# Three passes over groups of tokens become three phases over all tokens, and GpSimd normalises the probabilities

## The chip, the cores and the metric

One core of a Trainium2 chip. The metric is the device time of one execution in microseconds, the median of the runs shown.

## What is computed

One inference step of a one-layer streaming encoder in fp32: 2048 new frames of a prompt and 64 of a sample stream, model width 1024. 17 row tiles: 16 of 128 frames and one of 64.

```python
z = rms_norm(x, norm_mix) @ w_in            # 1024 -> 1408: u 256, q 768, k 192, v 192
d = trailing_means(u, (2, 4, 8, 16)) - u    # one window for each 64 channels
pool_o = (d @ w_pool_of_group) * pool_scale
q, k = rms_norm(q, q_norm), rms_norm(k, k_norm)        # by head of 64
s = q @ k.T / 8 - slope * abs(distance)     # 12 heads, 3 kv heads, 192 keys a chunk of 64
p = exp(s - m); p = p / (sum(p) + exp(sink - m))       # m = max(s, sink)
h = x + concat(pool_o, p @ v) @ w_out       # 1024 -> 1024
hn = rms_norm(h, norm_ffn)
y = h + (silu(hn @ w_gate) * (hn @ w_up)) @ w_down     # 1024 -> 2816 -> 1024
```

The last 15 rows of u and 128 rows of k and v are outputs too.

## The kernel before

Each fp32 operand of a large product is split in two fp32r numbers, high and low, and `split_products` (L601 to L603) issues three matmuls: high by high, high by low, low by high. ScalarE makes the high part of a weight block (`high1`, `high2`, L962, L967, L973), GpSimd the low part (`low`, L521), each for a block of 128 x 1024.

The tokens are cut in three parts of 768, 768 and 576 (`NT`, 6, 6 and 5 tiles). A part goes through everything before the next begins. `boundary` normalises its rows (ScalarE sums of squares, L991 to L995; VectorE scaling, L1325), transposes them on TensorE (L615) and splits them. `slab_unit` multiplies 11 slabs of `w_in` with the weights stationary and half the tokens of the part (384 or 288) moving, so that queries and keys come out transposed. Their sums of squares over a head are matmuls with a block of ones (`head_sums`, L679, L683, L684), values are transposed back (L658). Pooling windows are sums on GpSimd (L546, L550), mapped by `pool_map` (L742).

`attend` runs through the units (kv head g, tile t) in an order written out by hand. Of a unit: `scores` (L698), bias and maximum on VectorE (`softmax_top`, L1458 to L1473), exponentials with their sums on ScalarE (`exps`, L1108, L1110), sum, reciprocal and product on VectorE (`normalised`, L1483 to L1488), `prob_transposes` (L711), `weighted_values` (L727). Between the units lie late query slabs and tiles of the out projection (`out_tile`), whose products of 512 columns are added to `h` by VectorE (L1337).

The feed-forward is 11 groups of 256 columns of the hidden layer. A group is eight gate and up products of 24 matmuls (weights stationary, 384 or 288 tokens moving) and a down product with activations stationary and 512 columns of `w_down` moving: six matmuls for each full tile and half, four for the sample tile. Every part loads and splits all weights anew. Loads are issued by SyncE, stores of `h` by ScalarE.

## Time and profile before

| | before |
|---|---|
| median of 3 runs | 2288.44 us (2283.53 to 2292.7) |
| the profiled execution, its own time | 2288.89 us |
| its span | 2287.1 us |
| busy TensorE / VectorE / ScalarE / GpSimd | 97% / 41% / 32% / 27% |
| granted TensorE clock, mean | 0.99 |

The page lists the busy time of each engine (PE is TensorE, PEld its weight load, DVE VectorE, ACT ScalarE, POOL GpSimd, SP SyncE). A group line names a line of the kernel, the engine and operation, out<-in with shapes, the count, busy time and mean, and the idle time before them with what ended it. Matmuls are pipelined: one lasts longer than the step from its start to the next start. A window line gives for a stretch its length, the busy time of each engine with the count of instructions, the granted clock, and what the DMA engines moved.

### The profile page before, as it was taken

The numbers are of one execution on the slowest core, as the hardware profiler recorded it, in microseconds if no ns is written. First come the engines' busy times: TensorE is split into PE (matmuls) and PEld (weight loads), VectorE is DVE, ScalarE is ACT, GpSimd is POOL, SyncE is SP. The second block draws the span as 40 slices with busy tenths as digits, with TensorE's granted clock in tenths as the row PEclk, the third lists the DMA queues.
The fourth block names the chain that finished last, engine by engine and source line by source line (L and its number), as shares of the span: only waits on it lengthen the run. The fifth ranks groups of instructions, "written<-read, shape, count | busy, mean of one in ns | idle before, by whom it ended". The sixth has DMA issues, their size and how long they took to land.

```text
span 2287.1 us, 32537 instructions
## 1 busy us (share of the span) xinstructions
PE 2219.1 (97%) x12823; PEld 1998.9 (87%) x12823; DVE 948.6 (41%) x1589; ACT 726.0 (32%) x1570; POOL 625.2 (27%) x278
## 2 busy tenths in 40 slices
PE   7999999999999999999999999999998999999999
PEld 6876899999999989767999999999886689999998
DVE  3478613322222344786123322222557653434244
ACT  4565422121121235653212121121365342222221
POOL 2320333232232213102423232232132124333331
PEclk9999999999999999999999999999999999999999
DMA  4100232212112033002322212111321223223221
GB/s 135 47 34 20 90 99 61 68 55 73 55 55 92 19 129 102 19 20 92 96 70 64 65 56 73 55 58 53 115 94 38 82 74 102 83 74 91 73 74 42
DMA packets 194793, 159.94 MB, mean 70 GB/s; under 512 B 7421, under 2 KB 177322, under 8 KB 194698
## 3 DMA queue, kind: packets, MB, share of 16 engines
q1 hardware_dynamic: 191742, 149.55, 21.0%
q10 hardware_dynamic: 2956, 9.08, 1.0%
q8 instruction: 66, 1.08, 0.2%
q14 instruction: 29, 0.24, 0.0%
HBM read 149.63 MB, written 9.07 MB: 69 GB/s over the span
## 4 chain that ended last, share of the span: by engine, by line
PE 86%; DVE 8%; ACT 3%; issue 1%; DMA 1%; POOL 1%; SPq 0%; DVEq 0%; ACTq 0%
PE ps L601 27%; PE ps L602 26%; PE ps L603 26%; PE ps L727 2%; DVE xn L1325 1%; DVE s_sb L1458 1%; PE ps L698 1%; DVE negmax L1466 1%; PE ps L711 1%; DVE h L1337 1%; POOL w_lo L521 1%; ACT s_sb L1108 1%; DVE xt_lo L1316 1%; ACT xn L991 1%; PE ps L615 1%
## 5 line engine op out<-in xcount | busy, mean ns | idle before, releaser
L521 POOL TENSOR_TENSOR w_lo<-raw,w_hi 128x1024 fp32r<-128x1024 f32 x249 | 593.4, 2402 | 1571.4 <-ACT w_hi L973 961.5
L601 PE MATMUL ps<-xt_hi,w_hi 128*128 128x384 f32 (+1 forms) x2640 | 861.1, 326 | 4.0 <-DVE h L1337 1.9
L602 PE MATMUL ps<-xt_lo,w_hi 128*128 128x384 f32 (+1 forms) x2640 | 854.7, 324 | 0.0
L603 PE MATMUL ps<-xt_hi,w_lo 128*128 128x384 f32 (+1 forms) x2640 | 854.6, 324 | 0.0
L601 PEld LDWEIGHTS ps<-xt_hi,w_hi 128*128 128x128 f32 x2640 | 498.7, 189 | 13.0 <-issue 6.4
L602 PEld LDWEIGHTS ps<-xt_lo,w_hi 128*128 128x128 f32 x2640 | 498.7, 189 | 2.2
L603 PEld LDWEIGHTS ps<-xt_hi,w_lo 128*128 128x128 f32 x2640 | 498.3, 189 | 0.0
L1337 DVE TENSOR_TENSOR h<-ps,h 128x512 f32<-128x512 f32 (+1 forms) x510 | 349.8, 689 | 262.5 <-PE ps L603 261.2
L1555 DVE TENSOR_TENSOR aa<-ps,sg 128x384 f32<-128x384 f32 (+1 forms) x132 | 69.2, 524 | 826.7 <-PE ps L603 824.9
L601 PE MATMUL ps<-w_hi,act_hi 128*128 128x512 f32 x704 | 278.6, 396 | 0.0
L603 PE MATMUL ps<-w_hi,act_lo 128*128 128x512 f32 x704 | 277.8, 395 | 0.0
L602 PE MATMUL ps<-w_lo,act_hi 128*128 128x512 f32 x704 | 277.8, 395 | 0.0
L1195 ACT ACTIVATE sg<-ps 128x384 f32<-128x384 f32 (+1 forms) x132 | 61.4, 465 | 665.0 <-PE ps L603 664.9
L973 ACT ACTIVATE w_hi<-raw 128x1024 fp32r<-128x1024 f32 x150 | 150.5, 1049 | 65.0 <-PE ps L603 34.4
L967 ACT ACTIVATE w_hi<-raw 128x1024 fp32r<-128x1024 f32 x60 | 60.2, 1051 | 340.9 <-PE ps L603 248.2
L603 PEld LDWEIGHTS ps<-w_hi,act_lo 128*128 128x128 f32 x704 | 132.0, 187 | 31.9
L601 PEld LDWEIGHTS ps<-w_hi,act_hi 128*128 128x128 f32 x704 | 132.0, 188 | 30.2
L602 PEld LDWEIGHTS ps<-w_lo,act_hi 128*128 128x128 f32 x704 | 132.0, 188 | 30.2
L1568 DVE TENSOR_TENSOR act_lo<-aa,act_hi 128x384 fp32r<-128x384 f32 (+1 forms) x132 | 124.2, 941 | 2.8
L1108 ACT ACTIVATE s_sb<-s_sb,negmax 128x192 f32<-128x192 f32 (+1 forms) x198 | 86.7, 439 | 64.0 <-DVE esink L1473 63.6
L1209 ACT ACTIVATE act_hi<-aa 128x384 fp32r<-128x384 f32 (+1 forms) x132 | 64.8, 491 | 119.3 <-DVE aa L1555 119.3
L601 PE MATMUL ps<-w_hi,xt_hi 128*128 128x512 f32 x192 | 79.9, 416 | 4.0 <-POOL w_lo L521 4.0
(139 smaller groups left out, 1719.2 us busy)
## 6 DMA issues: line engine op xcount, KB each, us to landing
raw<-in_w_gate SPq DMA_DIRECT2D x66, 512.0 KB, 3.8
raw<-in_w_up SPq DMA_DIRECT2D x66, 512.0 KB, 3.9
raw<-in_w_down SPq DMA_DIRECT2D x66, 512.0 KB, 3.2
...
```

What stands on the lines that cost most here:

```text
L521: nc.gpsimd.tensor_tensor(lo, raw, hi.bitcast(F32), ALU.subtract).then_inc(done, 1)
L601: nc.tensor.matmul(out, w_hi, m_hi, start=first, stop=False)
L602: nc.tensor.matmul(out, w_hi, m_lo, start=False, stop=False)
L603: return nc.tensor.matmul(out, w_lo, m_hi, start=False, stop=last)
L967: nc.scalar.activation(w1_hi[:, c], raw1[:, c], ACT.Copy).then_inc(hi_done, 1)
L973: nc.scalar.activation(w2_hi[:, n], raw2[:, n], ACT.Copy).then_inc(hi_done, 1)
L1108: nc.scalar.activation(p, p, ACT.Exp, bias=negmax[:, b, e, c:c + 1], accum_out=den[:, b, e, c:c + 1])
L1195: nc.scalar.activation(sg[:, n % 2, 0:s.NB], ps[:, bank0 if n == 0 else 4 + n % 2, 0:s.NB], ACT.Silu).then_inc(silu_done, 1)
L1209: nc.scalar.activation(act_hi[:, parity, n // 2, (n % 2) * s.NB:(n % 2 + 1) * s.NB], aa[:, n % 2, 0:s.NB], ACT.Copy).then_inc(ah_done, 1)
L1337: nc.vector.tensor_tensor(out, ps[0:rows, bank, :], out, ALU.add).then_inc(d_free, 1)
L1555: nc.vector.tensor_tensor(aa[:, n % 2, 0:s.NB], ps[:, bank0 if n == 0 else 6 + n % 2, 0:s.NB], sg[:, n % 2, 0:s.NB], ALU.mult).then_inc(a_ ...
L1568: nc.vector.tensor_tensor(act_lo[at], aa[:, n % 2, 0:s.NB], act_hi[at].bitcast(F32), ALU.subtract).then_inc(al_done, 1)
```

## The change

The kernel is written anew around three phases.

Mixer phase, over all 17 tiles, with `w_in` held in SBUF, loaded and split once, and scaled by `norm_mix` there. The transposed tokens of a tile are stationary and weights move: 256 columns for u (`pool_columns`), and 384 for the queries, key and value of one kv head (`group_columns`), the u columns once a tile and the others once a unit. 51 units in the order of `UNITS`, in 55 steps: in step n TensorE projects unit n, transposes the queries and key of n-1, multiplies values of n-4, scores n-1, and transposes probabilities of n-3. Head sums are a reduction on VectorE, the normalising is done on rows. The trailing means are products with constant bands (`pool_means`). Row sums of x for a later tile stand at the head of ScalarE's step. The division: VectorE forms sum and reciprocal, GpSimd multiplies. The mixer output is stored to DRAM, with rows of 512 bytes.

Out phase, by tile: load the mixer output and x, split, multiply with `w_out` (which takes the place of `w_in`, loaded once), add, store h, normalise, transpose and store the result to DRAM.

Feed-forward phase, in three parts of 704 tokens: moving halves of 352, five tiles of 128 rows and one of 64 in each part. Both tokens and h are loaded from DRAM; the groups and the splitting of weights are as before, each part again with all weights.

The core of the diff:

```diff
-NT = (6, 6, 5)
-TILE0 = (0, 6, 12)
-TMAX = 6 * PART
...
+NTILES = 17
+SAMPLE = 16
+QCOLS = 4 * HD
+GCOLS = QCOLS + 2 * HD
+TILE_SETS = [(0, 1, 2)] + [(t,) for t in range(3, 14)] + [(14, 15, 16)]
+UNITS = [(g, t) for tiles in TILE_SETS for g in range(N_KV) for t in tiles]
...
+HALF_AT = {t: (3 * t - 2, 3 * t - 1) for t in range(3, 13)} | {t: (2 * t + 10, 2 * t + 11) for t in range(13, 17)}
+STEPS = NU + 4
...
+PARTS = 3
+T = TOKENS // PARTS
+NB = T // 2
...
-            def head_sums(s, oi):
-                need(pe, ss_free, oi)
-                if s.whole(oi):
-                    pe.wait_ge(sq_ready, oi + 1)
-                    nc.tensor.matmul(ps[:, 2, 0:s.NB], headsum[:, :], sq[:, oi % 2, 0:s.NB],
-                                     start=True, stop=True).then_inc(ss_ready, 1)
-                    return
-                pe.wait_ge(sq_low, s.splits(oi) + 1)
-                nc.tensor.matmul(ps[:, 2, 0:s.NB], headsum_r[:, :], sq_hi[:, 0:s.NB], start=True, stop=False)
-                nc.tensor.matmul(ps[:, 2, 0:s.NB], headsum_r[:, :], sq_lo[:, 0:s.NB],
-                                 start=False, stop=True).then_inc(ss_ready, 1)
...
-            def normalised(s, n):
-                t = s.units[n][1]
-                ai, chunks = s.a0 + n, s.chunks(t)
-                b = ai % 3
-                dve.wait_ge(e_ready, ai + 1)
-                link(nc.vector.tensor_tensor(den[:, b, :, 0:chunks], den[:, b, :, 0:chunks], esink[:, b, :, 0:chunks],
-                                             ALU.add))
-                link(nc.vector.reciprocal(rden[:, b, :, 0:chunks], den[:, b, :, 0:chunks]))
-                for c0, c1, k0 in s.spans(t):
-                    p = s_sb[:, b, :, KEYS * c0:KEYS * c1].rearrange("p e (c k) -> p e c k", k=KEYS)[:, :, :, k0:]
-                    last = nc.vector.tensor_tensor(
-                        p, p, rden[:, b, :, c0:c1].unsqueeze(3).to_broadcast([PART, 2, c1 - c0, KEYS - k0]), ALU.mult)
-                last.then_inc(p_ready, 1)
...
+            def load_mixed(i):
+                slot = (NTILES + i) % 3
+                if i < 3:
+                    sp.wait_ge(z_ready, ZG[UNIT[2, NTILES + i - 3]] + 1)
+                else:
+                    sp.wait_ge(out_ready, 2 * (i - 3) + 2)
+                for r, count in stored_at(i):
+                    sp.wait_ge(o_stored[r], 16 * count)
+                rows = rows_of(i)
+                load(xt_raw[:, slot, :, 0:rows], mix_k[:, :, PART * i:PART * i + rows], mix_loaded[i % 3])
...
+            def normalised(n):
+                t, b = UNITS[n][1], n % 3
+                pool.wait_ge(rden_ready, n + 1)
+                for c0, c1, k0 in spans(t):
+                    p = s_sb[:, b, :, KEYS * c0:KEYS * c1].rearrange("p e (c k) -> p e c k", k=KEYS)[:, :, :, k0:]
+                    last = nc.gpsimd.tensor_tensor(
+                        p, p, rden[:, b, :, c0:c1].unsqueeze(3).to_broadcast([PART, 2, c1 - c0, KEYS - k0]), ALU.mult)
+                last.then_inc(p_ready, 1)
+            for n in range(NU):
+                normalised(n)
+                for i in range(2):
+                    if n == 1:
+                        scale_group(2, i)
+                    if n == 2:
+                        wg_low(2, i)
+                for part, unit in enumerate([UNIT[g, SAMPLE] for g in (0, 0, 1)]):
+                    if n == unit + 1:
+                        for c in ((0, 1), (2, 3, 4), (5, 6, 7))[part]:
+                            wo_low(c)
+                if n >= NU - 2:
+                    mix_low(n - NU + 2)
+            mix_low(2)
...
+            def split_products(out, s_hi, s_lo, m_hi, m_lo, first, final):
+                nc.tensor.matmul(out, s_hi, m_hi, start=first, stop=False)
+                nc.tensor.matmul(out, s_lo, m_hi, start=False, stop=False)
+                return nc.tensor.matmul(out, s_hi, m_lo, start=False, stop=final)
...
+            def project(zi, t, w_hi, w_lo, cols, split):
+                out = bank_of_z(zi)[0:rows_of(t), 0:cols]
+                pe.wait_ge(tp_free, TP["x", t, 1] + 1)
+                rows, slot = rows_of(t), t % 3
+                for k in range(KT):
+                    if t == 0:
+                        pe.wait_ge(split, k + 1)
+                    last = split_products(out, xt_hi[:, slot, k, 0:rows], xt_lo[:, slot, k, 0:rows], w_hi[:, k],
+                                          w_lo[:, k], k == 0, k == KT - 1)
+                last.then_inc(z_ready, 1)
...
+            def query_transposes(n):
+                rows = rows_of(UNITS[n][1])
+                bank = tp_bank(("q", n))
+                pe.wait_ge(qn_ready, n + 1)
+                for i in range(3):
+                    last = nc.tensor.transpose(bank[:, rows * i:rows * (i + 1)], qn[0:rows, n % 2, PART * i:PART * (i + 1)],
+                                               ident[0:rows, 0:rows])
+                last.then_inc(tp_ready, 1)
...
+            def pool_means(t):
+                rows = rows_of(t)
+                pe.wait_ge(u_free, t + 1)
+                if t == 1:
+                    pe.wait_ge(band_loaded, 16)
+                need(pe, b3_free, B3["mean", t])
+                before = 3 if t == SAMPLE else (t - 1) % 3
+                for b in range(2):
+                    for e in range(2):
+                        i = 2 * b + e
+                        out = ps[HD * e:HD * (e + 1), 3, PART * b:PART * b + rows]
+                        f = slice(HD * i, HD * (i + 1))
+                        last = nc.tensor.matmul(out, u_sb[:, t % 3, f], band[:, i, 0:rows], start=True, stop=t == 0)
+                        if t > 0:
+                            last = nc.tensor.matmul(out, u_sb[:, before, f], prev[:, i, 0:rows], start=False, stop=True)
+                last.then_inc(b3_ready, 1)
...
+            def out_half(i, nh):
+                rows, slot = rows_of(i), (NTILES + i) % 3
+                pe.wait_ge(mix_split, i + 1)
+                if i == 0:
+                    pe.wait_ge(qn_ready, NU)
+                need(pe, out_free, 2 * i + nh - 1)
+                out, cols = ps[0:rows, nh], slice(512 * nh, 512 * (nh + 1))
+                for c in range(KT):
+                    if i + nh == 0:
+                        pe.wait_ge(wo_split, c + 1)
+                    hi, lo, _ = wo(c)
+                    last = split_products(out, xt_hi[:, slot, c, 0:rows], xt_lo[:, slot, c, 0:rows], hi[:, cols],
+                                          lo[:, cols], c == 0, c == KT - 1)
+                last.then_inc(out_ready, 1)
...
+            pe.wait_ge(ident_loaded, 16)
+            for t in range(3):
+                for half in range(2):
+                    x_transposes(t, half)
+                pool_columns(t)
+            cache_transposes()
+            pe.wait_ge(const_loaded, 16 * N_CONST)
+            for n in range(STEPS):
+                if n < NU:
+                    if n > 0:
+                        for t in pool_before(n):
+                            pool_columns(t)
+                    group_columns(n)
+                else:
+                    out_half((n - NU) // 2, (n - NU) % 2)
+                if 1 <= n <= NU:
+                    query_transposes(n - 1)
+                if n >= 4:
+                    weighted_values(n - 4)
+                if 1 <= n <= NU:
+                    scores(n - 1)
+                for e in step_events(n)[1]:
+                    if e[0] == "map":
+                        pool_map(e[1])
+                if 3 <= n < NU + 3:
+                    prob_transposes(n - 3)
+                for e in step_events(n)[1]:
+                    if e[0] == "mean":
+                        pool_means(e[1])
+                for e in step_events(n)[0]:
+                    if e[0] == "x":
+                        x_transposes(*e[1:])
+                if n >= STEPS - 2:
+                    x_transposes(NTILES, n - STEPS + 2)
+            for i in range(2, NTILES):
+                for nh in range(2):
+                    out_half(i, nh)
+                    x_transposes(NTILES + i - 1, nh)
+            for n in range(4):
+                for which in range(2):
+                    gate_up_unit(0, n // 2, n % 2, which)
+                if n < 2:
+                    x_transposes(2 * NTILES - 1, n)
+            pe.wait_ge(out_free, 2 * NTILES)
+            pe.wait_ge(tp_free, len(TP_EVENTS))
+            for G in range(1, NG):
+                gate_up(G)
+                down(G - 1)
+            down(NG - 1)
...
+            for n in range(STEPS):
+                for t in HALF_AT:
+                    if x_step(t) == n:
+                        x_rstd(t)
+                if 0 < n < NU:
+                    for t in pool_before(n):
+                        pool_copy(t)
+                if n < NU:
+                    squares(n)
+                if 1 <= n <= NU:
+                    query_copy(n - 1)
+                if n < NU:
+                    value_copy(n)
+                    head_rstd(n)
+                if n >= 4:
+                    output_copy(n - 4)
+                for e in step_events(n)[1]:
+                    if e[0] == "map":
+                        map_copy(e[1])
+                if 3 <= n < NU + 3:
+                    prob_copy(n - 3)
+                for e in step_events(n)[1]:
+                    if e[0] == "mean":
+                        means_copy(e[1])
+                for e in step_events(n)[0]:
+                    if e[0] == "x":
+                        x_high(*e[1:])
+                if n in (1, 2, 4, 5):
+                    wg_highs(1 + n // 4, (n - 1) % 3)
+                for part, unit in enumerate([UNIT[g, SAMPLE] for g in (0, 0, 1)]):
+                    if n == unit + 2:
+                        wo_highs(part)
+                if NU - 1 <= n < NU + 2:
+                    mix_highs(n - NU + 1)
+                if 1 <= n <= NU:
+                    exps(n - 1)
+                if n == STEPS - 2:
+                    h_rstd(0)
+                if n >= STEPS - 2:
+                    stage_copy(0, n - STEPS + 2)
+            for i in range(2, NTILES + 1):
+                h_rstd(i - 1)
+                if 3 <= i + 1 < NTILES:
+                    mix_highs(i + 1)
+                if i == 4:
+                    high2(0, range(4))
+                if 9 <= i < NTILES:
+                    xb_highs(0, i - 9)
+                for half in range(2):
+                    stage_copy(i - 1, half)
...
+            for n in range(STEPS):
+                for t in HALF_AT:
+                    if x_step(t) == n:
+                        x_norm(t)
+                if 0 <= n - 2 < NU:
+                    normalised(n - 2)
+                if n < NU:
+                    head_sums(n)
+                    normed(n)
+                else:
+                    out_add((n - NU) // 2, (n - NU) % 2)
+                if 1 <= n <= NU:
+                    softmax_top(n - 1)
+                for e in step_events(n)[0]:
+                    if e[0] == "x":
+                        x_low(*e[1:])
+                if n in (1, 2):
+                    wg_lows(1, n - 1)
+                if n == STEPS - 2:
+                    h_norm(0)
...
+            def normalised(n):
+                t = UNITS[n][1]
+                b, nch = n % 3, chunks(t)
+                dve.wait_ge(e_ready, n + 1)
+                link(nc.vector.tensor_tensor(den[:, b, :, 0:nch], den[:, b, :, 0:nch], esink[:, b, :, 0:nch], ALU.add))
+                nc.vector.reciprocal(rden[:, b, :, 0:nch], den[:, b, :, 0:nch]).then_inc(rden_ready, 1)
...
```

## Rows read from the trace of the kernel before

**Rows 1.** the page, part 1: busy time of each engine

```profile
PE 2219.1 (97%) x12823; PEld 1998.9 (87%) x12823; DVE 948.6 (41%) x1589; ACT 726.0 (32%) x1570; POOL 625.2 (27%) x278
```

**Rows 2.** timeline of TensorE in feed-forward groups: start us, us, engine, line

```profile
359.62 0.34 PE L601 MATMUL ps<-xt_hi,w_hi 128*128 128x384 f32 x1
...
392.90 0.39 PE L601 MATMUL ps<-w_hi,act_hi 128*128 128x512 f32 x1
...
409.70 0.34 PE L601 MATMUL ps<-xt_hi,w_hi 128*128 128x384 f32 x1
...
2099.91 0.30 PE L602 MATMUL ps<-xt_lo,w_hi 128*128 128x288 f32 x1
...
2100.84 0.30 PE L603 MATMUL ps<-xt_hi,w_lo 128*128 128x288 f32 x1
```

**Rows 3.** groups by line and form: count, busy us, mean ns, idle before

```profile
L601 PE MATMUL ps<-xt_hi,w_hi 128*128 128x384 f32 x1760 | 598.2, 340 | 2.4 <-issue 1.2 <-DVE h L1337 1.1
...
L601 PE MATMUL ps<-w_hi,act_hi 128*128 128x512 f32 x704 | 278.6, 396 | 0.0
...
L601 PE MATMUL ps<-xt_hi,w_hi 128*128 128x288 f32 x880 | 262.9, 299 | 1.7 <-DVE h L1337 0.8 <-issue 0.6 <-POOL w_lo L521 0.2
```

**Rows 4.** timeline of TensorE, one unit of attention between out products

```profile
1001.61 0.92 PE L698 MATMUL ps<-kt_sb,qt_sb 64*128 64x192 f32 x8
1002.46 0.87 PE L711 MATMUL ps<-ident,s_sb 128*128 128x128 f32 x6
1003.27 1.39 PE L727 MATMUL ps<-pt_sb,v_sb 64*64 64x128 f32 x16
1004.59 0.50 PE L601 MATMUL ps<-w_hi,xt_hi 128*128 128x512 f32 x1
```

**Rows 5.** timeline of TensorE, a whole head sum and what follows it

```profile
109.22 0.91 PE L679 MATMUL ps<-sq,headsum 128*128 128x384 f32 x2
109.97 0.60 PE L711 MATMUL ps<-ident,s_sb 128*64 128x128 f32 x4
```

**Rows 6.** windows: length, busy (count) of PE PEld DVE ACT POOL, PEclk, DMA, GB/s

```profile
0.00:295.00 295.00, 267.50 (x1588) 226.13 (x1589) 172.37 (x316) 150.82 (x389) 64.44 (x38) 0.98 0.22 68
1630.00:1880.00 250.00, 225.42 (x1492) 189.49 (x1491) 150.65 (x299) 119.81 (x334) 57.99 (x27) 0.96 0.26 83
128.00:138.00 10.00, 10.00 (x47) 8.46 (x48) 7.81 (x22) 5.72 (x23) 2.18 (x1) 0.53 0.28 105
10.00:20.00 10.00, 5.62 (x24) 4.70 (x24) 8.13 (x8) 7.40 (x17) 6.16 (x4) 1.00 0.81 259
```

**Rows 7.** timeline of the start

```profile
3.96 1.06 ACT L991 ACTIVATE xn<-h 128x1024 f32<-128x1024 f32 x1 [1.78 <-DMA h<-in_x_prompt]
...
5.47 0.20 ACT L995 ACTIVATE rstd<-ss 128x1 f32<-128x1 f32 x1
...
10.69 1.94 PE L615 MATMUL ps<-ident,xn 128*128 128x128 f32 x8 [10.69 <-DVE xn L1325]
...
12.30 1.28 DVE L1325 SCALAR_TENSOR_TENSOR xn<-h,rstd,g_mix 128x1024 f32<-128x1024 f32 x1 [1.76 <-ACT rstd L995]
...
14.80 2.35 POOL L521 TENSOR_TENSOR w_lo<-raw,w_hi 128x1024 fp32r<-128x1024 f32 x1
...
14.89 3.34 DVE L1325 SCALAR_TENSOR_TENSOR xn<-h,rstd,g_mix 128x1024 f32<-128x1024 f32 x1
```

**Rows 8.** timeline of one softmax on VectorE and ScalarE

```profile
1008.54 1.14 DVE L1458 SCALAR_TENSOR_TENSOR s_sb<-dist,slope,ps 128x384 f32<-128x384 f32 x2 [0.17 <-PE ps L698]
...
1011.10 0.46 ACT L1108 ACTIVATE s_sb<-s_sb,negmax 128x192 f32<-128x192 f32 x1
...
1012.87 0.19 ACT L1110 ACTIVATE esink<-esink 128x4 f32<-128x4 f32 x1
```

**Rows 9.** groups by line and form, the low part on GpSimd and the normalising

```profile
L521 POOL TENSOR_TENSOR w_lo<-raw,w_hi 128x1024 fp32r<-128x1024 f32 x249 | 593.4, 2402 | 1571.4 <-ACT w_hi L973 961.5 <-ACT w_hi L962 343.3 <-ACT w_hi L967 266.3
...
L1488 DVE TENSOR_TENSOR s_sb<-s_sb,rden 128x768 f32<-128x768 f32 x45 | 48.1, 1069 | 1.6
```

2043 lines of the change are left out of this document (831 added, 1212 removed).

## The prediction

> **What bounds the kernel now.** I read the page first: TensorE is busy for 2219.1 us of the span of 2287.1, and no other engine reaches half of it [rows 1]. So the end is set by the TensorE stream, and two things are wanted: what the stream needs, and what is lost in it. Busy time is no measure of need, since matmuls overlap; the step from one start to the next is. In a feed-forward group of parts 1 and 2, 192 matmuls of 384 columns run from 359.62 to 392.90 and 72 of 512 columns from there to 409.70, without an idle record between them [rows 2]: 173.3 and 233.3 ns each. In part 3 seven steps of 288 columns take 0.93 us, 133 ns. The line through 288 and 384 is 0.42 ns a column plus 12.5 ns; it gives 160 ns at 352 and 120 ns at 256 columns (estimates). The counts are those of the grouping by form [rows 3], each for one of three products.
>
> By these steps the feed-forward of before needs 22 groups of 50.1 us and 11 of 38.7 (192 x 133 ns + 56 x 233.3 ns): 1527.8 us. The other 759 us are three mixers with out projection. Their stream: 1056 x 173.3 + 528 x 133 ns = 253 us of projection, 800 x 233.3 ns = 187 us of out projection; attention, by one step of tile and group: scores, probability transposes, weighted values from 1001.61 to 1004.59, 2.98 us [rows 4], 45 full units and 6 smaller ones (2.4 and 1.55 us) 146 us; 34 row tiles of eight transposes at some 0.93 us (six take 0.81), 32 us; head sums of 0.75 us a whole unit of 384 columns [rows 5], 27 whole and 21 split ones, 26 us; pooling map, value and state transposes, some 15 us. Sum 2186. So about 101 us are lost. In the windows over the mixers TensorE is idle for 27.5 us in part 1 and 24.6 in part 3, and its granted clock is 0.98 and 0.96 on the mean, 0.53 from 128 to 138 us, which is the 1.2 GHz level after short pauses [rows 6]. The feed-forward loses nothing. A better time can only come from these 101 us, and each new matmul costs its step.
>
> **The change part by part: the stream.** Feed-forward, gate and up: 6336 matmuls of 352 columns instead of 4224 of 384 and 2112 of 288, 1014 us each way; nothing. Down: five full tiles and one of 64 rows in each part are 68 matmuls a group, 33 x 68 = 2244 against 2200: +10.3 us. Out projection 17 x 48 = 816 against 800, since the sample tile loses its short form: +3.7. Projection: tokens are now stationary and weights move, 51 x 24 of 384 columns and 17 x 24 of 256: 212.1 + 49.0 = 261.1 us, +8; the sample tile pays full columns. Queries and keys come out in rows, so the head-sum matmuls go (-26) and so do value and state transposes (-6.5), and three transposes a unit come: six take 0.81 us [rows 4], so 0.43 x 51 = +22. Pooling means move from GpSimd to eight small matmuls a tile, half of the sixteen that take 1.32 us [rows 4], with the switch 0.75 x 17 = +13. The map costs the same. Together the stream is 2186 + 25 = 2211 us.
>
> One rule of the Trainium skill speaks on the steps. "TensorE: Matmul & The Clock Gate", section "Back-to-back issue gap", gives columns / 2.4 + 2.5 ns for a single warm matmul and says that real streams are set by weight load and matmul together. The row shows 173.3 ns at 384 columns where the formula has 162.5, so the measurement decides; by the formula the 256-column matmuls would take 109 instead of 120 ns, and the sum would be 4.5 us lower.
>
> **What is lost in the new stream.** (a) Start. Now TensorE starts at 10.69 us, because the first row scaling waits for a broadcast weight [rows 7]; the new one needs none (the weight goes into w_in), so the transposes can start near 7. But then ScalarE has, in order, three row sums of 1.7 us (3.96 to 5.67), 8 + 8 weight copies, and copies of transposes, and VectorE the same number of low parts. By their durations the first group matmul comes at some 28 us, of which 11 are needed: 17 lost (12 to 25, as the copies overlap or not). The loads for it, 4 MB, take about 16 us at the 259 GB/s of rows 6 and lie beside it. (b) Filling the pipeline over nine steps, with group 1 and 2 weights still being split: 7. (c) Steady steps. The loop is scores, bias and maximum on VectorE (2.52 us from 1008.54), exponentials on ScalarE (1011.10 to 1013.06) [rows 8], then in ScalarE's order the squares of the next unit (0.4), the query copies (0.6), scores (0.97): 6.5 us, and 7.0 when the normalising of queries, which VectorE now does ahead of the bias, is late. TensorE needs 7.6 us a step (24 x 173.3 ns + 0.43 + 2.98) and 28 for a tile's three steps with pooling, so it covers the loop. Once a tile the row sum of a later tile (1.7 us) and its scaling (1.28) stand at the head of a step: 9.5 us against 8. Some 1 us a tile, 14 in all; bounds 0 (pool columns cover it) and 45 (3 us a tile, if durations add end to end instead of overlapping by 0.09 us as between copies). (d) The end of the mixer. Five w_out splits of 0.96 us stand ahead of the exponentials of one step, three of another: 6. The first low part of the stored mixer output is queued on GpSimd behind the multiply of unit 49, whose divisors need scores, bias and exponentials of that unit: 4.5 + 0.4 + 1.5 + 2.4 us after its scores, while TensorE is ready after 0.8: 8 lost. Bounds 3 and 25. (e) Out phase. A tile is 11.2 us of products and 1 of transposes; 2 MB go and come in it (mixed rows, residual, two stores), 164 GB/s. A load issued at the tile's start lands after some 7 us behind the stores, then 1.05 on ScalarE and 2.4 on GpSimd: 11, hidden by 12.2. Around the load of the first feed-forward part (2.9 MB) and the first weights it is not: 5 in all, bounds 0 and 40. (f) Entry of the feed-forward: gates wait on ScalarE behind the last staging copies (3), and group 1 has no down work ahead of it, so its first split, issued behind 4 MB of loads, comes 5 us late: 8, bounds 3 and 20. (g) Last matmul to end, now 6 us, stays 6. (h) Each long pause is followed by a stretch at 1.2 GHz [rows 6]: two such, 5, and 2 for small gaps, less than before has of both since the gaps at each change of kind are in the unit times, taken from start to start. Bounds 3 and 25.
> Together 17 + 7 + 14 + 14 + 5 + 8 + 6 + 7 = 78, hence a span of 2211 + 78 = 2289 us, against 101 lost in 2287. With the 1.8 us around the span of the profiled run (2288.89), 2291 us; that run and the median shown (2288.44) agree. Weights of w_in and w_out are loaded once instead of three times, and their splitting leaves GpSimd; both are hidden, and bring nothing.
>
> **GpSimd's multiply.** VectorE gives up 1.07 us a unit, GpSimd takes it at 2.4 ns an element in the nearest row [rows 9]: 1.8 us for 768 (VectorE's 1.07 is the floor, the 2.4 of a whole block of 1024 the ceiling). Divisors are ready 0.4 us after the exponentials, in the next step; the transposes that want the result stand a step later, over 8 us on. Hidden, and queued behind it are only weight splits.
>
> **Rivals.** Faster (2265): the 26 us of (b), (c) and (e) vanish since 28 us of TensorE work a tile cover all of it. For it: ScalarE has about 17 us a tile, VectorE 15. Against: the order within ScalarE, where a row sum stands ahead of squares. Slower, by the softmax loop (2325): if the loop takes 8.7 us a step instead of 7.0, two of a tile's three steps, those without pool columns, are longer than TensorE's 7.6 by 1.1: 17 x 2.2 = 37 more, less the 1 a tile that is in the sum already where both fall together. It decides above 7.6 us. For it: in part 3 of before, with least work beside attention, TensorE is idle 24.6 us [rows 6]. Slower, by collisions (2330): a VectorE operation with two SBUF inputs that starts beside a GpSimd one takes 3.34 us instead of 1.28 [rows 7], 2.06 more, about as long as the GpSimd operation runs. The Trainium skill has it so ("GPSIMD Engine Reference", section "Key points": the two share SBUF interfaces, with contention when VectorE uses two SBUF inputs). In the new mixer GpSimd runs once a step, and the maximum against the sinks has two SBUF inputs; it lies 4.5 us after the divisors in my order and misses the 1.8 us. If the multiply lasts over 4 us, each step is late by about 0.8: 51 x 0.8 = 40. Slower, by transfers (2330): if stores and 512-byte reads share less than 164 GB/s, at 140 each out tile costs 2 us more, 15 x 2 = 30, and the entry 10. Against: 259 GB/s in rows 6. That the change does not do what it says: the multiply is not on the path where I place it, so even a serial one shows only if it decides above 8 us.
>
> **How the numbers follow.** The forecast is no change worth naming, 2291: chance 0.38 that it stays within 0.5%, 2277 to 2300 (0.5% is about what this kernel's measurement can tell). The faster rival 0.25. Softmax loop 0.17, collisions 0.07, transfers 0.10, multiply or order not as read 0.03: slower 0.37. The bounds of (c) to (f) above carry 31, 11, 35 and 12 us up, not all at once: 2330 as the upper end; with (b), (c) and (e) gone and 5 less at the start it is 2260.
>
> **What would show it.** Feed-forward group steps of 46.6 us (33 x 46.6 = 1538) show the stream right. Gate steps of 160 ns, group projection 24 steps of 173, pool 120. TensorE idle in the first 30 us near 17 less or more; in steady mixer tiles a period near 29 us for three steps; a wait for a GpSimd low part of 8 us at the first out tile; out tiles of 12.2 us; one wait for weights at the second feed-forward group. Wrong would be: projections with moving weights off the line, a mixer tile over 31 us, waits of TensorE for GpSimd's product in every step, or a lower granted clock through the mixer.

## The result, and the profile after

The changed kernel takes 2344.56 us (median of 4 runs, 2342.04 to 2348.61) against 2287.78 for the kernel before, measured beside it: 1.0249 times as long, 95% interval 1.0223 to 1.0275. Slower by 2.5%, 54 us over the predicted 2291 and above the range's end of 2330. Measured a second time, the same pair came out at 1.0198 (1.018 to 1.0217), 2340.1 against 2295.9; so the two measurements of one pair differ by 0.5%. Times of experiments are set against this second 2340.1. They were taken on several chips, on which the kernel before took 2291.5 to 2295.9 us, so a difference of less than some 5 us needs the ratio or the trace beside it.

The page of the profiled execution (span 2339.8 us), its busy times and its line of the granted clock in 40 slices:

```profile
PE 2241.1 (96%) x13246; PEld 2040.4 (87%) x13246; DVE 808.6 (35%) x1446; ACT 727.3 (31%) x1781; POOL 653.9 (28%) x311
PEclk9899999998999999999999999999999999999999
```

Against [rows 1], TensorE is busy 22 us longer and the span is 52.7 longer, so 31 us more are idle. The windows of the changed kernel, cut at its stages, show where. Columns as in [rows 6]: length, busy of PE, PEld, DVE, ACT, POOL, then clock, DMA share and GB/s.

```profile
0.00:29.40 29.40, 16.43 (x100) 15.46 (x100) 14.03 (x28) 17.20 (x38) 1.41 (x6) 0.94 0.73 203
29.40:112.50 83.10, 68.72 (x463) 61.20 (x461) 42.95 (x101) 46.79 (x164) 21.04 (x14) 0.90 0.23 66
112.50:418.30 305.80, 284.12 (x2224) 250.21 (x2225) 134.87 (x329) 180.63 (x613) 44.04 (x30) 0.99 0.12 35
418.30:550.20 131.90, 111.99 (x864) 95.71 (x862) 60.49 (x139) 75.02 (x247) 38.58 (x22) 0.94 0.18 59
550.20:786.20 236.00, 219.38 (x1016) 174.64 (x1016) 37.77 (x57) 89.01 (x231) 61.02 (x29) 0.95 0.51 163
786.20:861.20 75.00, 67.34 (x395) 66.45 (x394) 10.21 (x18) 18.34 (x38) 14.12 (x6) 0.93 0.40 116
861.20:2339.80 1478.60, 1473.12 (x8197) 1376.67 (x8195) 508.25 (x776) 300.30 (x453) 473.72 (x204) 1.00 0.25 80
```

They are: the start; nine steps that fill the pipeline; ten steady tiles (3 to 12); the last tiles and the end of the mixer; the out projection; the two gate and up groups that enter the feed-forward; the rest. The last is as good as full. All that went wrong lies before 861 us. What TensorE waited for, in total (waited-for tile and line; us, times, longest):

```profile
PE ps L655 <- DVE xt_lo L1216: 22.2, 13, 2.1
PE ps L655 <- POOL xt_lo L576: 18.4, 4, 12.7
PE ps L725 <- ACT kt_sb L981: 15.4, 16, 2.6
PE ps L669 <- DVE xn L1207: 11.1, 3, 7.1
PE ps L669 <- ACT wg_lo_raw L1056: 7.7, 3, 4.5
PE ps L655 <- POOL w_lo L576: 4.8, 1, 4.8
PE ps L655 <- POOL wg_lo L600: 4.0, 1, 4.0
PE ps L770 <- DMA band<-in_c_band: 3.9, 1, 3.9
PE ps L655 <- ACT sg L1089: 2.9, 1, 2.9
```

The first row was in no term of the prediction's sum. One of its 13 instances, in the timeline of the changed kernel (start, duration):

```profile
264.10 0.60 PE L669 MATMUL ps<-ident,xn 128*128 128x128 f32 x4
264.30 0.81 ACT L1002 ACTIVATE pt_sb<-ps 128x768 f32<-128x768 f32 x1
265.01 0.59 ACT L939 ACTIVATE xt_hi<-ps 128x512 fp32r<-128x512 f32 x1
265.63 0.69 DVE L1216 TENSOR_TENSOR xt_lo<-ps,xt_hi 128x512 fp32r<-128x512 f32 x1
266.47 0.36 PE L655 MATMUL ps<-wu_hi,xt_hi 128*128 128x256 f32 x1 [1.77 <-DVE xt_lo L1216]
```

The second transposed half of x is the last thing TensorE does in a step (264.10), and the pool columns that open the next step read it. Between lie ScalarE's copy of the probabilities, its high part and VectorE's low part: 1.77 us of waiting. In the step before that one TensorE waits another 0.53 us for the transposed keys (L725 <- L981). The period of a tile is 30.50 us.

The second row is the end of the mixer, again in the timeline:

```profile
536.92 6.95 POOL L576 TENSOR_TENSOR wg_lo<-wg_lo_raw,wg_hi 128x1024 fp32r<-128x1024 f32 x3
537.23 2.13 DVE L1241 TENSOR_TENSOR k_st<-qn,kgrow 64x64 f32<-64x64 f32 x1
541.63 2.26 DVE L1267 TENSOR_TENSOR esink<-negmax,sink 128x4 f32<-128x4 f32 x1
546.37 1.47 POOL L618 TENSOR_TENSOR s_sb<-s_sb,rden 128x768 f32<-128x768 f32 x1 [2.50 <-DVE rden L1275]
547.80 2.34 POOL L576 TENSOR_TENSOR xt_lo<-xt_lo_raw,xt_hi 128x1024 fp32r<-128x1024 f32 x1
550.19 0.80 PE L655 MATMUL ps<-wu_hi,xt_hi 128*128 128x512 f32 x1 [12.68 <-POOL xt_lo L576]
```

Three weight low parts (7 us) come first; beside them VectorE's sum of sinks and negated maximum, 4 elements wide, takes 2.26 us where it takes 0.16 alone (265.38 in the trace). So the divisors are late, then the multiply (GpSimd stands idle for 2.50 us between its block of weight parts and the multiply), then the low part of the first mixed tile, and TensorE stands for 12.68 us.

### The profile page after: what moved, and what is told of

It is laid out like the page before. It is cut to its first block, busy times and chain, and to the rows that moved or that the text cites. A ratio compares the mean times of both kernels' runs of the same rounds, so it can differ in the third digit from the quotient of the medians.

```text
span 2339.8 us, 32102 instructions
## 1 busy us (share of the span) xinstructions
PE 2241.1 (96%) x13246; PEld 2040.4 (87%) x13246; DVE 808.6 (35%) x1446; ACT 727.3 (31%) x1781; POOL 653.9 (28%) x311
## 4 chain that ended last, share of the span: by engine, by line
PE 89%; ACT 5%; DVE 3%; DMA 1%; issue 1%; POOL 1%; SPq 0%; ACTq 0%; DVEq 0%; POOLq 0%
PE ps L655 27%; PE ps L657 26%; PE ps L656 26%; PE ps L751 2%; PE ps L725 2%; PE ps L841 1%; ACT s_sb L990 1%; PE ps L669 1%; PE ps L737 1%; DMA xt_lo_raw<-mix_d 1%; DVE s_sb L1253 1%; ACT xn L926 1%; PE ps L843 1%; PE ps L839 1%; DVE negmax L1261 1%
## 5 line engine op out<-in xcount | busy, mean ns | idle before, releaser
L576 POOL TENSOR_TENSOR w_lo<-w_lo_raw,w_hi 128x1024 fp32r<-128x1024 f32 x198 | 471.0, 2410 | 1042.8 <-ACT w_hi L1068 523.8
L655 PE MATMUL ps<-xb_hi,w_hi 128*128 128x352 f32 x2112 | 686.7, 325 | 7.7 <-POOL w_lo L576 4.8
L657 PE MATMUL ps<-xb_lo,w_hi 128*128 128x352 f32 x2112 | 684.8, 324 | 0.0
L656 PE MATMUL ps<-xb_hi,w_lo 128*128 128x352 f32 x2112 | 683.8, 324 | 0.0
L655 PEld LDWEIGHTS ps<-xb_hi,w_hi 128*128 128x128 f32 x2112 | 398.2, 189 | 9.4 <-issue 8.0
L656 PEld LDWEIGHTS ps<-xb_hi,w_lo 128*128 128x128 f32 x2112 | 400.1, 189 | 1.2
L657 PEld LDWEIGHTS ps<-xb_lo,w_hi 128*128 128x128 f32 x2112 | 397.5, 188 | 0.0
L655 PE MATMUL ps<-wg_hi,xt_hi 128*128 128x384 f32 (+3 forms) x612 | 224.4, 367 | 4.0 <-POOL wg_lo L600 4.0
L656 PE MATMUL ps<-wg_hi,xt_lo 128*128 128x384 f32 (+3 forms) x612 | 220.1, 360 | 0.0
L657 PE MATMUL ps<-wg_lo,xt_hi 128*128 128x384 f32 (+3 forms) x612 | 219.7, 359 | 0.0
```

The source lines that it names most:

```text
L576: nc.gpsimd.tensor_tensor(lo, raw, hi.bitcast(F32), ALU.subtract).then_inc(done, 1)
L655: nc.tensor.matmul(out, s_hi, m_hi, start=first, stop=False)
L656: nc.tensor.matmul(out, s_lo, m_hi, start=False, stop=False)
L657: return nc.tensor.matmul(out, s_hi, m_lo, start=False, stop=final)
```

## The experiments

**x one step earlier.** The edit to the changed kernel:

```diff
-HALF_AT = {t: (3 * t - 2, 3 * t - 1) for t in range(3, 13)} | {t: (2 * t + 10, 2 * t + 11) for t in range(13, 17)}
+HALF_AT = {t: (3 * t - 3, 3 * t - 2) for t in range(3, 13)} | {t: (2 * t + 10, 2 * t + 11) for t in range(13, 17)}
```

> The changed kernel with the transposed halves of x of token tiles 3 to 12 placed one step of the mixer earlier, so that the GpSimd and VectorE copies of the second half have a whole unit of attention before the window means read them. Nothing else is changed and no work is added. Theory A (the wait at the head of the third unit of each tile is the wait of the window means for the low part of x, 13 waits and 22.2 us in the changed kernel's trace, and it makes the wait for the transposed keys late too): both waits shrink, the period of a steady tile falls from 30.50 us to about 28.8, the stretch up to the out projection shortens by 20 to 30 us, and the whole time is 2315 to 2325 us. Rival B (TensorE waits there for the softmax loop of VectorE, ScalarE and GpSimd, and only the name of the last releaser is x): the period stays within 0.4 us of 30.5, the waits move to the probabilities or to other tiles, and the time stays at 2340 to 2348 us. Rival C (the earlier transposes need x sooner than its loads bring it): the steps at the start get longer by 5 us or more, and half of the gain or more is lost there.

Measured: 2311.92 us, 1.0059 (1.0042 to 1.0077) times the kernel before; 28.2 us less than the changed kernel. The window over the same ten tiles of this kernel:

```profile
107.80:386.50 278.70, 278.61 (x2227) 247.11 (x2225) 138.56 (x334) 181.12 (x616) 44.01 (x30) 1.00 0.13 39
```

and its timeline around the same transposes:

```profile
238.18 0.66 PE L669 MATMUL ps<-ident,xn 128*128 128x128 f32 x4
238.87 0.60 ACT L939 ACTIVATE xt_hi<-ps 128x512 fp32r<-128x512 f32 x1 [0.20 <-PE ps L669]
239.50 0.69 DVE L1216 TENSOR_TENSOR xt_lo<-ps,xt_hi 128x512 fp32r<-128x512 f32 x1 [0.56 <-ACT xt_hi L939]
246.55 0.36 PE L655 MATMUL ps<-wu_hi,xt_hi 128*128 128x256 f32 x1
```

The low part is done 6 us before it is read. TensorE is idle for 0.09 us in 278.7, at the full clock; the tile takes 27.90 us, the stretch is 27.1 us shorter. Theory A, and by more than it asked (28.8 us a tile, 2315 to 2325 in all); the wait for the keys in the steady tiles went with the other. No x came late: rival C is out. One edit in a placement table gave back 28 of the 44 us that the second measurement shows as lost.

**The multiply back on VectorE, and the multiply doubled.** One kernel has the multiply of line 618 on VectorE behind the reciprocal, as before the change; two do it twice on GpSimd:

```diff
-                for c0, c1, k0 in spans(t):
...
-                last.then_inc(p_ready, 1)
+                for turn in range(2):
+                    for c0, c1, k0 in spans(t):
...
+                    last.then_inc((once_done, p_ready)[turn], 1)
+                    pool.wait_ge((once_done, p_ready)[turn], n + 1)
```

> The changed kernel with the multiply by the reciprocal of the softmax sum back on VectorE, as in the kernel before; GpSimd waits for its result at the same place of its order. Everything else stays. Theory A (the place of the multiply is off TensorE's path in the steady tiles, and the loss there is x and the window means): the period of a steady tile stays within 0.3 us of 30.5 and the time within 10 us of 2344.6; GpSimd's busy time falls by about 54 x 1.33 = 72 us and VectorE's rises by about as much. Rival B (GpSimd's multiply of 1.47 us a unit, at the end of a chain of exponentials, reciprocal, multiply and split, is what makes the probabilities late): the time falls by 15 us or more, to 2330 us or less, with the period under 30.0 us. Rival C (VectorE is as full as GpSimd, and its operations with two operands in SBUF wait for GpSimd's): the period rises by 0.5 us or more a tile and the time goes over 2355 us.

> The changed kernel with GpSimd's multiply of the probabilities by the reciprocal of their sum done twice (the probabilities are divided twice, so the attention output is another one; all else is computed as before). Each unit's multiply takes 2.9 us instead of 1.47. Theory A (the multiply is hidden, and the steady tiles lose their time to x): the period of a steady tile stays at 30.5 us within 0.3, and the time rises by 1 to 5 us, at the end of the mixer. Rival B (the loop of the softmax through GpSimd sets the step): the period rises by up to 3 x 1.45 = 4.4 us a tile, and the time by 40 us or more.

> The same doubled multiply on the kernel with the transposed halves of x one step earlier (2311.9 us, period 27.90 us). Its probabilities too are divided twice. Theory A (also without the wait for x the multiply has more than 1.5 us of slack): the period stays at 27.9 us within 0.3, the time at 2312 to 2318 us. Rival B (the wait for x only hid that GpSimd is next): the period rises by 1 us or more a tile, the time by 12 us or more. Rival C (VectorE's operations with two operands in SBUF now meet the longer GpSimd work and wait for it): their mean duration grows by over 0.5 us and the period by 0.3 to 1.5 us.

Measured: on VectorE 2349.83 us, 1.0234 (1.0208 to 1.0261), 9.7 us above the changed kernel (by the ratios 8, and their intervals overlap by a little); steady tiles of 31.26 us, two of them 32.8, against 30.50. That is more than theory A allows (0.3) and less than rival C's total; rival B is out. Doubled: 2341.54 us (1.0214, interval 1.0186 to 1.0241), tiles of 30.50; doubled with x earlier 2311.0 us, tiles of 27.90. The group of the doubled multiply in this last kernel, and of the single one on VectorE (count | busy, mean ns | idle before):

```profile
L620 POOL TENSOR_TENSOR s_sb<-s_sb,rden 128x768 f32<-128x768 f32 x90 | 132.0, 1467 | 283.3 <-DVE rden L1278 279.7
```

```profile
L1273 DVE TENSOR_TENSOR s_sb<-s_sb,rden 128x768 f32<-128x768 f32 x45 | 45.0, 1000 | 1.6
```

Another 1.47 us a unit on GpSimd moves neither period, even where TensorE never waits, and VectorE's short sum of maximum and sinks keeps its mean (0.30 us for 0.32). So the multiply has 1.5 us of slack or more and is hidden as forecast; what it cost was another 1.2 us at the end of the mixer (first wait of the out phase 13.9 us for 12.7). Back on VectorE each tile is 0.8 us longer: TensorE then waits 0.7 us in nine steady tiles for a copy of the attention output by ScalarE, which it doesn't in the changed kernel. GpSimd's multiply is the one part of the change that was taken back alone, and it helps, as the kernel stands with x late; with x in time this wasn't tried.

**The end of the mixer.** The whole edit, then its halves:

```diff
-                    if n == unit + 1:
+                    if n == unit:
                         for c in ((0, 1), (2, 3, 4), (5, 6, 7))[part]:
                             wo_low(c)
-                if n >= NU - 2:
-                    mix_low(n - NU + 2)
-            mix_low(2)
+                if n >= NU - 3:
+                    mix_low(n - NU + 3)
```

> The changed kernel with two moves in GpSimd's order of work at the end of the mixer: the low parts of the out projection's weight are made one unit earlier, and the low part of the mixer's first output tile is made two places earlier, ahead of the multiply of the last unit. Theory A (the out projection's first wait of 12.7 us for the low part of the mixed tile is GpSimd's order: three weight low parts of 7 us stand ahead of it and delay the last units' multiply): the wait falls to 5 us or less, the time falls by 6 to 10 us, to 2335 to 2339 us. Rival B (the wait is set by the last output tile itself, its copy and its loads, and the weight parts only look as if they were ahead): the wait stays at 10 us or more and the time within 3 us of 2344.6. Rival C (the three weight parts now delay an earlier unit's probabilities by as much): the first wait of the out projection falls, but the last tile of the mixer gets longer by 5 us or more, and the time stays within 3 us.

> One half of the edit of the mixer's end, alone: the low parts of the first mixed tiles are made one place earlier in GpSimd's order (the first ahead of the multiply of the last unit); the weight's low parts stay where the changed kernel has them. The whole edit gave 2321.5 us against 2340.1. Theory A (the low part of the mixed tile stands in a queue behind the last unit's multiply, and that multiply is late because GpSimd's weight parts hold up VectorE): the first wait of the out projection falls from 12.7 to 5 or 6 us, and with the clock the time falls by 10 to 16 us, to 2324 to 2330. Rival B (the weight parts ahead are what matters, and the tile's low part can't start before them): the wait falls by no more than 3 us and the time by no more than 5.

> The other half alone: the low parts of the out projection's weight one unit earlier, the low parts of the first mixed tiles where the changed kernel has them. Theory A (they end as a block of 7 us ahead of the last unit's multiply; one unit earlier, that block is off the last unit's way): the first wait falls to 7 to 10 us and the time by 4 to 10, to 2330 to 2336. Rival B (VectorE's small operations wait for whichever weight part is running, so that moving the block moves the delay with it): VectorE's operations with two operands in SBUF still last up to 1.5 or 2.3 us at their new places, and the time falls by no more than 4 us.

Measured: both 2321.53 us (1.0112, interval 1.0086 to 1.0138), 18.6 us less; mixed tile alone 2327.8 (1.0155, 1.0136 to 1.0174), weight parts alone 2335.3 (1.0194, 1.0175 to 1.0213). The waits for this low part with both edits, and with the mixed tile's alone:

```profile
PE ps L654 <- POOL xt_lo L576: 5.9, 4, 4.7
```

```profile
PE ps L654 <- POOL xt_lo L576: 9.7, 3, 8.7
```

The first wait is 12.7, 8.7 with the mixed tiles alone, 9.7 with the weight parts alone and 4.7 with both, so each edit takes off its own part (4.0 and 3.0 of 8.0). The time shows this less clearly: the weight parts alone are 4.8 us below the changed kernel, but by the ratios (1.0194 against 1.0198) nothing is left of it. The gain of both is twice what was expected. In the changed kernel the second output tile waits as well (4.5 us; 5.3 in its second run), since its low part is queued the same way; moving the mixed tiles removed that, and the weight parts alone did not (4.5). So the queue on GpSimd is the cause, of two waits instead of one, and theory A is right on the whole edit. On the halves it is right in part: with the mixed tiles moved alone the wait should have fallen to 5 or 6, and with the weight parts moved VectorE's short operations still last 1.0 to 1.5 us at their new places, as rival B had it.

**GpSimd's block in smaller pieces.**

```diff
-                low(wo_high, c + 1, lo, raw, hi, wo_split)
+                pool.wait_ge(wo_high, c + 1)
+                for q in range(4):
+                    cols = slice(256 * q, 256 * (q + 1))
+                    last = nc.gpsimd.tensor_tensor(lo[:, cols], raw[:, cols], hi[:, cols].bitcast(F32), ALU.subtract)
+                last.then_inc(wo_split, 1)
```

> The changed kernel with each low part of the out projection's weight on GpSimd done in four operations of 256 columns instead of one of 1024 (four times some 0.6 us instead of 2.35 us), in the same order. The changed kernel alone: 2340.1 us. Theory A (VectorE's operation waits until the GpSimd operation beside it has ended, so a shorter one holds it up less, and this is what makes the last units' multiply late): VectorE's operations of 2.1 to 2.3 us at the end of the mixer fall to 0.8 us or less, the first wait of the out projection falls from 12.7 us by 2 to 4, and the time falls by 2 to 5 us. Rival B (only the block ahead of the multiply counts): the VectorE operations get shorter but the wait stays within 1 us of 12.7. Rival C (four small operations cost GpSimd more than one, 0.1 us each or more): the block grows from 7 to 8 us or more and the wait grows.

> The version of 2269.8 us (x one step earlier, mixer's end, loads first, entry of the feed-forward) with the low parts of the out projection's weight in four operations each. Theory A (shorter GpSimd operations hold VectorE up less): the remaining first wait of 4.6 us falls by 1 to 2 us, and the time to 2266 to 2269 us. Rival B (nothing left there depends on it): within 1 us of 2269.8.

Measured: 2340.59 us (1.0208, 1.0181 to 1.0235), no change; on the best version 2268.83, no change either. The timeline with pieces (the first three lines at an earlier block, the last at the one ahead of the first wait):

```profile
515.65 8.32 POOL L614 TENSOR_TENSOR wg_lo<-wg_lo_raw,wg_hi 128x256 fp32r<-128x256 f32 x12
520.24 5.19 DVE L1270 TENSOR_TENSOR negmax<-negmax,nsink 128x2 f32<-128x2 f32 x1
523.95 1.46 POOL L622 TENSOR_TENSOR s_sb<-s_sb,rden 128x768 f32<-128x768 f32 x1
541.81 0.65 DVE L1271 TENSOR_TENSOR esink<-negmax,sink 128x4 f32<-128x4 f32 x1
```

The VectorE operation on the path fell from 2.26 to 0.65 us as theory A says, but the block grew from 7.0 to 8.3 us (538.29 to 546.54 for the last) and the multiply then starts at its end: first wait 11.4 us instead of 12.7, time the same. Both rivals hold a part. And shorter operations are no sure cure: at 520.24 a VectorE operation of two columns lasted 5.19 us, to 525.43, when GpSimd's chain of pieces and the multiply behind them (523.95 + 1.46 = 525.41) was over. What the collisions cost at this end: from the block's start to the divisors it is 9.4 us in the changed kernel (536.92 to 546.30) and 7.1 with the pieces (538.29 to 545.41), so some 2.3 us (the 2.50 us of GpSimd's idle time above are the most it can be), and the 1.3 us of longer block plus the multiply's place behind it gave most of that back.

**The idle stretch filled.** 52 matmuls of no use where TensorE waits:

```diff
-                pe.wait_ge(mix_split, i + 1)
...
+                if i + nh == 0:
+                    pe.wait_ge(wo_split, 1)
+                    for _ in range(52):
+                        nc.tensor.matmul(ps[:, 0], wo(0)[0][:, 0:PART], wo(0)[0][:, 0:512], start=True, stop=True)
+                pe.wait_ge(mix_split, i + 1)
```

> The changed kernel with 52 matmuls of 512 columns, of no use to the result, put on TensorE where it waits 12.7 us for the first mixed tile's low part: 52 x 0.227 = 11.8 us, so that the wait is filled and nothing else changes. Theory A (the idle stretch costs more than its own length: the granted clock falls to half for part of the first tiles after it, 0.84 over the 54.6 us behind it, where it is 0.91 when the wait is short): the end of the mixer stays where it is, the first out tiles run at the full clock, and the time falls by 4 to 9 us, to 2331 to 2336. Rival B (the clock falls for what stands around, not for that idle stretch, or it falls all the same): within 3 us of 2340. Rival C (the filler ends late and delays the first tile): up to 5 us slower.

Measured: 2338.59 us, 1.0207 (1.0189 to 1.0225): the ratio is above the changed kernel's second one, the time below it, so no difference that the runs can tell, and not the 4 to 9 us of theory A. The first output half (24 matmuls) ran in 5.66 us at a granted clock of 1.00, instead of 7.23 at 0.78; behind the 4.75 us wait the next halves still took 7.2 us, at 0.77 and 0.76 (7.8 us at 0.70 and 0.71 in the changed kernel's second run). So the pause does cost the half behind it 1.6 us, and filling it didn't bring the halves behind the next pause to the full clock.

**Loads ahead of stores in the out phase.**

```diff
-                store_h(i - 1) if i > 2 else (store_h(0), store_h(1))
-                store_hn(i - 2)
-                if 3 <= i + 1 < NTILES:
+                if i > 2 and i + 1 < NTILES:
                     load_mixed(i + 1)
                     load_residual(i + 1)
+                if i == 2:
+                    store_h(0)
+                    load_mixed(3)
+                    load_residual(3)
+                    store_h(1)
+                else:
+                    store_h(i - 1)
+                store_hn(i - 2)
```

> The changed kernel with the loads of the next tile's mixed values and residual issued ahead of the stores of h and of the normalised h on SyncE's queue, in the out projection phase. Theory A (the waits of 7.7 us for the weight's raw part and of 5.7 us beyond the first for the mixed low part come from loads that stand behind stores which wait for VectorE): the tiles of the out phase shorten by 4 to 8 us together, and the time falls to 2336 to 2341 us. Rival B (these waits come from the band of the DMA queues, shared with the feed-forward's weights, and the order on the queue makes no difference): the phase stays at 236 us within 3, and the time at 2341 to 2348 us. Rival C (the stores get later, and the feed-forward's first tile waits for them): the step into the feed-forward gets longer by 3 us or more.

Measured: 2329.39 us (1.0146, 1.012 to 1.0173), 10.7 us less. The waits for the staging copy:

```profile
PE ps L675 <- ACT wg_lo_raw L1062: 0.8, 1, 0.8
```

7.7 us of waits became 0.8, and the output phase fell from 237.8 us (second run of the changed kernel) to 225.6: 7 by the waits, some 4 because the two halves behind them run in 5.55 to 5.58 us instead of 8.2 and 7.2. Theory A, by more than it asked (2336 to 2341), with the clock on top; the band of the queues is not the cause, since the same bytes go in 12 us less.

**The order of the three products.** After, the stationary low part multiplies second; before, the moving one does. One kernel each way:

```diff
-                nc.tensor.matmul(out, s_lo, m_hi, start=False, stop=False)
-                return nc.tensor.matmul(out, s_hi, m_lo, start=False, stop=final)
+                nc.tensor.matmul(out, s_hi, m_lo, start=False, stop=False)
+                return nc.tensor.matmul(out, s_lo, m_hi, start=False, stop=final)
```

> The changed kernel with the three products of each step in the order of the kernel before: high by high, high by low, then low by high; the same number of matmuls, the same operands. Theory A (the order of the products sets the step between 512-column matmuls: 226.7 ns on the average in the changed kernel against 233.4 ns in the kernel before): the down steps go to about 233 ns, which over 7 x 2112 / 22 = 672 plus the out projection's 816 512-column matmuls, and all those of the down projection, 3168 together, is 20 us; the time rises by 14 to 25 us. Rival B (the average differs because of what stands around, not because of the order): steps and time stay within 5 us. Rival C (the order before is better for the 256- and 352-column groups): the time falls by 5 us or more.

> The kernel before with the three products of a step in the order of the changed kernel: high by high, low by high, then high by low. Theory A (the order sets the 512-column step): the kernel before gains, its 512-column steps fall from 233.4 to about 227 ns, and its time falls by 10 to 20 us, so that a part of what the change has in its favour is the order alone. Rival B (the order is worth nothing): within 4 us of the kernel before. Rival C (the matmuls of the other widths get longer by as much): within 4 us, with steps moved both ways.

Measured: 2342.06 us (1.02, 1.0182 to 1.0219) beside 2340.09 for the changed kernel; 0.9997 (0.9985 to 1.0009) for the kernel before. A down group takes 15.46 us in the one and 16.80 in the other as it did. Rival B both times: the order is worth nothing, and theory A was a wrong reading of a real difference (227 against 233 ns a 512-column step). The traces at hand spoke against it: in the changed kernel the halves of the out phase take 232 ns a step with the new order, and in the kernel before the last down group takes 227 with the old one. From the first of these rows to the second are 48 steps:

```profile
2268.71 0.39 PE L601 MATMUL ps<-w_hi,act_hi 128*128 128x512 f32 x1
2279.61 0.39 PE L755 MATMUL ps<-w_hi,act_hi 128*128 128x512 f32 x1
```

So both steps occur in both kernels; what picks one of them stays open.

**All together.** The changed kernel once more, beside three edits at once, and then the entry of the feed-forward too:

> The changed kernel once more, unaltered, beside the others of this call, so that they can be compared on one chip. Theory: 2340 to 2352 us, and 1.022 to 1.027 times the kernel before; if the ratio is below 1.02, the chip matters to the comparison and the differences among kernels of one call are the ones to use.

> The changed kernel with the three edits tried one by one put together: the transposed halves of x one step earlier, the low parts of the out projection's weight and of the first mixed tile earlier in GpSimd's order, and the next tile's loads ahead of the stores in the out phase. Theory A (the three losses are apart from each other and add up, as 33, 23 and 15 us against 2344.6): 2344.6 - 71 = 2274 us, 2268 to 2282, which is faster than the kernel before. Rival B (the first two repair the same end of the mixer, and the loads give back only what the clock had lost): 2285 to 2300 us, no better than the kernel before. Rival C (the transfers, with the mixer shorter by some 40 us, come late for the out phase): its tiles wait for data for 10 us or more and the time is over 2300 us.

```diff
-                if n < 2:
-                    x_transposes(2 * NTILES - 1, n)
+                    if n == 0:
+                        x_transposes(2 * NTILES - 1, which)
...
+                    if G == 0 and n == 3:
+                        high2(1, range(2))
...
-                high2(G + 1, range(4 if G + 1 < NG else 2))
+                high2(G + 1, range(2 if G == 0 else 0, 4 if G + 1 < NG else 2))
```

> The combined kernel of 2279.0 us with two edits at the entry of the feed-forward: the transposes of the last token tile both stand by the first gate and up units, so that ScalarE has done with its copies before the first gate is ready, and two of the four weight matrices of the second group are copied by ScalarE ahead of the fourth gate. Theory A (the 2.9 us wait for the gate's activation and the 4.9 us for the weight's low part are the order of ScalarE's work): both go, and the time falls by 5 to 9 us, to 2270 to 2274. Rival B (the second group's weights come that late from their loads): the 4.9 us stay or go over to the fourth gate, and the time falls by 2 to 3 us. Rival C (the table of the activation is loaded at the same place whatever the order): the 2.9 us stay.

Measured: control 2340.09; three edits 2278.99 us, 0.993 (0.9912 to 0.9949); with the entry 2269.78 us, 0.9904 (0.9887 to 0.9922); with the pieces as well 2268.83, 0.99 (0.9874 to 0.9926), which is no further gain. Singly the three gave 28.2 + 18.6 + 10.7 = 57.5 us, together 61.1: they add up. The windows of the three-edit kernel at the same stages as above, from the fill on:

```profile
29.15:106.10 76.95, 65.90 (x463) 58.43 (x462) 41.38 (x97) 45.15 (x160) 21.05 (x14) 0.96 0.22 67
106.10:384.80 278.70, 278.61 (x2226) 247.10 (x2225) 138.65 (x334) 181.27 (x616) 44.06 (x30) 1.00 0.13 39
384.80:506.10 121.30, 111.93 (x863) 95.38 (x861) 56.74 (x136) 73.43 (x238) 37.25 (x21) 0.97 0.20 64
506.10:723.80 217.70, 212.78 (x1015) 170.53 (x1016) 37.77 (x61) 91.12 (x240) 62.83 (x30) 0.98 0.56 177
```

The entry edit took the wait for the gate's activation away and left 0.9 of the 4.9 us for the weight's low part; its 9.2 us by the times, 6 by the ratios and 7.9 by the spans of the profiled runs, are about both waits. So the matmuls of the changed kernel, every one in its three phases, run 1% faster than the kernel before, and the slowdown of the change is wholly one of placement.

## Why the prediction was wrong, point by point

By stage, with the losses of the forecast put where they belong. Its stream of 2211 less 1537.5 in the feed-forward and 209.3 in the out phase leaves 464 in the mixer, 11 of it in the start. The 209.3 are 816 x 233.3 ns, the transposes of sixteen tiles (11.8) and the last units' attention, 7.1 us by the trace, which runs in that window:

| stage | predicted | after | three edits |
|---|---|---|---|
| to the first group matmul | 28 | 29.4 | 29.2 |
| nine filling steps | 71 | 83.1 | 77.0 |
| ten steady tiles | 290 | 305.8 | 278.7 |
| rest of the mixer | 127 | 131.9 | 121.3 |
| out phase | 214 | 236.0 | 217.7 |
| feed-forward | 1546 | 1548.1 | 1546.5 |
| end, clock | 13 | 5.5 | 5.5 |

The last column but one adds up to 2339.8. The sum went wrong by 51 us, and nearly all in five terms.

*The stream* was right. In the feed-forward of the changed kernel

```profile
1000.70 0.39 PE L655 MATMUL ps<-w_hi,act_hi 128*128 128x512 f32 x1
1016.17 0.32 PE L655 MATMUL ps<-xb_hi,w_hi 128*128 128x352 f32 x1
1047.22 0.39 PE L655 MATMUL ps<-w_hi,act_hi 128*128 128x512 f32 x1
```

68 down matmuls take 15.47 us (227 ns each) and 192 of 352 columns 31.05 (161.7 ns): 46.52 us against 46.6. Two errors cancel: 1.7 ns x 6336 = 11 us more and 6 ns x 2244 = 13 us less. Steps of 173 and 120 ns for the projections came as drawn from [rows 2]: here measurement was the one to take, and not the formula that the Trainium skill gives for a single matmul ("TensorE: Matmul & The Clock Gate", "Back-to-back issue gap"; an estimate of 149.2 ns at 352 columns by it, for 161.7 measured). The prediction priced that formula at the 256 columns alone, 4.5 us. Over the 6336 matmuls of 352 columns it would, by the same estimate, have made the sum another 68 us lower, so more hung on this choice than was said. The clean steady tile of 27.90 us is the 28 of the text. The pooling means with the switch cost 1.07 us a tile and not 0.75: I took half of sixteen from [rows 4], and the trace shows sixteen. That is 5 us.

*(c), steady steps: 1 us a tile forecast, 2.6 measured, 27 us in these ten tiles for 10.* This is the step that failed first and cost most in the mixer. The price of the loop was right: TensorE covered it, and with x out of the way also a multiply twice as long. What I left out is a dependence: I put the transposes of x into the sum as work and asked only when ScalarE gets to the row sums. I never asked who reads the second half and how soon. The answer, the first matmul of the next step, is in the code: `HALF_AT` places the second half at the end of a step, and `pool_columns` opens the next. 1.8 us there and 0.5 to 0.6 for the keys behind it are the 2.5 us a tile. My bound of 45 us covered it; the value taken, 1 us a tile, had no row.

*(b), the fill: 7 forecast, 19 measured.* The waits are one each for GpSimd's low part of the projection weight (4.0), the table of the window means (3.9) and the low part of x (2.1), 3.8 for the keys, and the clock at 0.90. The table and x were in no term. With the x edit alone and no other it fell by about 3 us; the rest wasn't tried.

*(d), the end of the mixer: 8 us forecast for its wait, 12.7 measured, and a second wait of 4.5 of the same kind.* The queue was named rightly: the low part behind the multiply of the last unit. Missing were the weight low parts ahead of that multiply, and that the next tile meets the same queue.

*(e), the out phase: 5 forecast, 27 measured* (236.0 less 209.3), inside its bounds of 0 to 40. 5.7 are the further waits for a mixed tile's low part (4.5 of it the second wait of (d)), 7.7 loads behind stores on one queue, 3.2 the scaling of the first tile; five halves, behind these waits and the first of (d), took 6.7 to 8.3 us for 5.6, together some 10 more. I computed the landing at 11 us against 12.2 and called it hidden; a margin of 1.2 us on a queue shared with stores that wait for VectorE was no margin.

*(f), entry: 8 forecast, 12 measured* (75.0 less 384 x 161.7 ns = 62.1 and 0.75 of transposes). Both causes were named with their place, priced 3 and 5, and measured 2.9 and 4.8; the rest goes with a granted clock of 0.93, which is argued and not tried alone.

*(h), clock and small gaps: 7 forecast.* Taken by number of long pauses, two; there were more, because each failed term made one. The granted clock of the output phase was 0.95, 0.98 with the three edits. Removing waits of 7 us gave 10.7 and removing one of 8 with 4 or 5 behind it gave 18.6: here a pause cost its length and then some halves at 7.2 to 8.3 us for 5.6.

*The rivals.* The softmax loop (2325) is refuted by the x edit: with x in time TensorE is idle for 0.09 us in ten tiles, so a step of the loop is covered by its 27.90 us a tile. The doubled multiply says the same of the part through GpSimd alone; the loop as the prediction drew it doesn't hold the multiply. The collisions (2330) do occur, 2.26 us for 0.16, but they came from the weight low parts and not the multiply (1.47 us, where that rival needed 4), and are worth some 2 us there. That the trace agrees with the rule of the Trainium skill ("GPSIMD Engine Reference", "Key points") did not make it the bound. Transfers (2330) did cost, by the order in the queue and not the band. None of the three was the cause of 54 us, which was several places of 10 to 28 us each; the range's upper end assumed that they would not all come at once, and they did, in one direction. The faster case (2265) is near what the new stream can do, 2269, but not by its own sum: it had the losses of (b), (c) and (e) gone, and only (c) went. With the three edits the fill still loses 13 us and the out phase 8; what makes up for it are the 8 of (f), gone by the entry edit, and the 7 of (h), which lie in the stages. That the numbers meet is in part luck.
